# Decay and gate products in one visit, the unit's norm earlier, and matrices zeroed by GpSimd, in a two-block transformer kernel

## The reference, cut to what matters

```
r, k, v, z, wd, ad = split(token_shift(x @ w_in))
decay = exp(-exp(-softplus(-(w0 + tanh(wd) @ w_up)) - 0.5))   # decay: rank 64 up to 1024
a     = sigmoid(a0 + ad @ a_up)                               # gate: rank 64 up to 1024
kk    = normalized(k * k_k);   k = k * (1 + (a - 1) * k_a)
for t: sa = S a_t;  S = S * w_t + sa b_t + v_t k_t;  o_t = S r_t
o = (o - mean) * rsqrt(var + eps) * gn_w + gn_b               # the norm, head by head
o = (o + sum(r * k * r_k) * v) * silu(z)
```

## Time and profile before

| what | value |
|---|---|
| median of three runs | 3003.76 us (3002.83 to 3004.73) |
| the profiled execution's own time | 3004.44 us |
| its span | 3002.6 us |
| PE busy | 2942.5 us, 98% |
| DVE, ACT, POOL busy | 1686.2, 1247.3, 279.7 us |
| granted TensorE clock, mean | 0.994 |

### The profile page before, as it was taken

The page is one execution under the profiler, slowest core; times in us unless marked ns, Lnnn a source line. Parts: engine busy times, 40 slices in busy tenths (PEclk is TensorE's granted clock), DMA queues, the critical chain, the costliest instruction groups (busy, mean ns, idle before and its releaser), DMA issues.

```text
span 3002.6 us, 39945 instructions
## 1 busy us (share of the span) xinstructions
PE 2942.5 (98%) x15626; PEld 2367.6 (79%) x15626; DVE 1686.2 (56%) x3028; ACT 1247.3 (42%) x2193; POOL 279.7 (9%) x513
## 2 busy tenths in 40 slices
PE   8999999999999999999999999999999999999997
PEld 7878878787878887777778877877878787787886
DVE  6555555545453335565653346666666666666557
ACT  5444443434333325454443234343444434344322
POOL 0110100001000000000000002020120202023101
PEclk9999999999999999999999999999999999999999
DMA  4222222222233322222233323132222313126244
GB/s 171 79 85 78 85 78 84 84 79 84 80 124 134 119 97 72 77 72 71 71 109 140 128 92 93 57 95 73 83 87 71 100 57 101 62 88 204 80 153 155
DMA packets 86794, 289.16 MB, mean 96 GB/s; under 512 B 12096, under 2 KB 12864, under 8 KB 86352
## 3 DMA queue, kind: packets, MB, share of 16 engines
q1 hardware_dynamic: 71184, 246.42, 24.2%
q0 software_dynamic: 15424, 40.19, 4.4%
HBM read 261.26 MB, written 25.17 MB: 95 GB/s over the span
## 4 chain that ended last, share of the span: by engine, by line
PE 92%; DVE 4%; ACT 2%; issue 2%; DMA 0%; DVEq 0%; ACTq 0%
PE bank L283 18%; PE bank L285 17%; PE bank L284 17%; PE bank L287 7%; PE bank L289 7%; PE bank L288 7%; PE bank L1383 2%; PE bank L340 1%; PE bank L320 1%; PE bank L1292 1%; PE bank L469 1%; PE bank L482 1%; PE bank L1313 1%; PE bank L1320 1%; ACT mc_split L566 1%
## 5 line engine op out<-in xcount | busy, mean ns | idle before, releaser
L283 PE MATMUL bank<-ma_split,mc_split 128*128 128x512 f32 x2304 | 954.6, 414 | 22.9 <-DVE mb L1807 14.2
L736 DVE TENSOR_TENSOR mc_split<-mc,mc_split 128x1024 fp32r<-128x1024 f32 x434 | 534.8, 1233 | 766.4 <-ACT mc_split L566 765.6
L285 PE MATMUL bank<-ma_split,mc_split 128*128 128x512 f32 x2304 | 904.3, 392 | 0.0
L284 PE MATMUL bank<-ma_split,mc_split 128*128 128x512 f32 x2304 | 902.0, 391 | 0.0
L566 ACT ACTIVATE mc_split<-mc 128x1024 fp32r<-128x1024 f32 x434 | 457.2, 1055 | 583.7 <-PE bank L287 321.3
L283 PEld LDWEIGHTS bank<-ma_split,mc_split 128*128 128x128 f32 x2304 | 435.1, 189 | 132.9 <-issue 58.4
L285 PEld LDWEIGHTS bank<-ma_split,mc_split 128*128 128x128 f32 x2304 | 434.0, 188 | 96.1
L284 PEld LDWEIGHTS bank<-ma_split,mc_split 128*128 128x128 f32 x2304 | 436.1, 189 | 80.0 <-issue 5.5
L287 PE MATMUL bank<-mc_split,ma_split 128*128 128x512 f32 x576 | 232.0, 403 | 4.0 <-DVE mb L1807 2.4
L289 PE MATMUL bank<-mc_split,ma_split 128*128 128x512 f32 x576 | 225.5, 392 | 0.0
L288 PE MATMUL bank<-mc_split,ma_split 128*128 128x512 f32 x576 | 225.1, 391 | 0.0
(11 more groups left out here) (366 smaller groups left out, 3605.4 us busy)
## 6 DMA issues: line engine op xcount, KB each, us to landing
mc<-in_w SPq DMA_DIRECT2D x434, 512.0 KB, 3.6
x<-mc POOLq DMA_DIRECT2D x8, 1024.0 KB, 5.2
y<-mb_split SPq DMA_DIRECT2D x28, 256.0 KB, 2.6
ma_split<-y POOLq DMA_DIRECT2D x28, 256.0 KB, 4.6
mb<-in_xt SPq DMA_DIRECT2D x8, 512.0 KB, 8.9
mc<-in_x POOLq DMA_DIRECT2D x4, 1024.0 KB, 5.5
mc<-x POOLq DMA_DIRECT2D x4, 1024.0 KB, 7.7
mats<-mc POOLq DMA_DIRECT2D x32, 128.0 KB, 2.2
```

The source lines that it names most:

```text
L283: mm = pe.matmul(banks[j][:], wh[:, c], act_hi[:, kt, :], start=(kt == kts[0]), stop=False)
L284: pe.matmul(banks[j][:], wl[:, c], act_hi[:, kt, :], start=False, stop=False)
L285: last = pe.matmul(banks[j][:], wh[:, c], act_lo[:, kt, :], start=False, stop=(kt == kts[-1]))
L736: dve.tensor_tensor(w_low[:, s % NR, :, :], w_raw[:, s % NR, :, :], w_high[:, s % NH, :, :].bitcast(F32), ALU.subtract).then_inc(w_lo, 1)
```

## The change

Four edits:

1. Step k = 0 of a unit issues both products, decay into bank 7 and gate into bank 4; step k = 1 keeps only ACT's part, which reads bank 4.
2. The state's U product goes to columns 256 to 383 of bank 6 in place of bank 4, which frees bank 4 for the gate.
3. The norm's steps 36 to 41 of units 0 to 6 stand at points 164, 167, 175, 180, 183 and 186 in place of 178, 181, 184, 187, 190 and 193. For the last HGRN head, steps up to m = 8 take the other heads' spacing of 4.5 points, and the later ones stand 4 points behind where they stood.
4. `m8` is zeroed by GpSimd at the start of its second program, behind a wait for the row norms (`rb_ready`), in place of DVE in unit 0.

```diff
-                return begin + 178 + 3 * (i - CHUNK_K)
+                return begin + (164, 167, 175, 180, 183, 186)[i - CHUNK_K]
             def hg_at(h, m):
-                return 128 * h + 65 + m * (40 if h == UNITS - 1 else 45) // 10
+                if h == UNITS - 1 and m > 8:
+                    return 128 * h + 101 + 4 * (m - 8)
+                return 128 * h + 65 + 9 * m // 2
...
-            D_BANK = banks[7]
+            D_BANK, A_BANK = banks[7], banks[4]
...
-                CHUNK += [(f"R{c}", 6, "act")] * (c > 0) + [(f"U{c}", 4, "dve"), (f"O{c}", 5, "act")]
+                CHUNK += [(f"R{c}", 6, "act")] * (c > 0) + [(f"U{c}", 6, "dve"), (f"O{c}", 5, "act")]
...
-            C_BANK = {name: banks[b] for name, b, _ in CHUNK if b}
+            C_BANK = {name: banks[b][:, 2 * P:3 * P] if name[0] == "U" else banks[b] for name, b, _ in CHUNK}
...
-                if ("rw", k) in D_USES:
+                if ("rw", k) in D_USES and k != 1:
                     d_claim(pe, "rw", u, k)
-                if k in (0, 1):
+                if k == 0:
                     if u == 0:
                         pe.wait_ge(wa_ready, 2)
-                    rank = slice(k * RANK, (k + 1) * RANK)
-                    pe.matmul(D_BANK[:], up[rank, cols], wa[rank, :], start=True, stop=True).then_inc(d_done, 1)
+                    for i, bank in enumerate((D_BANK, A_BANK)):
+                        rank = slice(i * RANK, (i + 1) * RANK)
+                        pe.matmul(bank[:], up[rank, cols], wa[rank, :], start=True, stop=True).then_inc(d_done, 1)
...
-                    act.activation(asg, D_BANK[:], ACT.Sigmoid, bias=pc[A0]).then_inc(d_free, 1)
+                    act.activation(asg, A_BANK[:], ACT.Sigmoid, bias=pc[A0]).then_inc(d_free, 1)
...
-                        dve.memset(m8, 0.0).then_inc(m8_zeroed, 1)
...
             def second_pool(pool):
+                pool.wait_ge(rb_ready, 3)
+                pool.memset(m8, 0.0).then_inc(m8_zeroed, 1)
                 pool.wait_ge(m8_zeroed, 1)
```

## The result

The changed kernel takes 2962.34 us, the median of four runs (2958.5 to 2964.83), against 3004.24 us for the kernel before (3002.83 to 3006.88). The ratio is 0.9858, with a 95% interval of 0.9841 to 0.9875: 42 us faster. The forecast was 2970 us with a range from 2965.5 to 2982. The profiled execution took 2963.0 us, its span is 2961.2 us.

The account below looks back on a forecast made before the run. The prediction took TensorE, busy 98% of the span, as the bound: its instructions plus its holes. Terms of 9.1 + 17.7 + 1.0 + 4.4 + 3.1 - 1.2 = 34.1 us gave 2970 us, range 2965.5 to 2982.

Parts of the forecast that it names:

- decay and gate together: In 8 units, one visit for both products costs what one did, saving 1.14 us each: 9.1 us gained.
- holes at seven block ends: At seven hg block ends, the earlier norm closes TensorE's 2.52 us wait for emptied banks: 17.7 us gained.
- the wait of L1241 behind them: TensorE's wait for the fourth bank, four times, 2.0 us in all, mostly closes: 1.0 us gained.
- unit 0: Without DVE's 3.47 us memset, the waits of L1262 and L1241 in unit 0 go: 4.4 us gained, lower end 2.3.
- last head's product: L1383's 2.9 us wait for L1828 at the last head closes with its step 4 points later: 3.1 us gained.
- wait for the inverses: TensorE waits up to 0.5 us for GpSimd's inverses in each of units 1 to 6: 1.2 us lost.
- rival of three passes: Strict program order makes the merged visit one pass longer: 4.2 us, 2974.5 us; half or no overlap together 0.09.
- the walk: New order traced through hg block 3: emptying starts near 2234.6, bank 0 free near 2235.3, about 0.5 us to spare.
- late-split rival: At block ends the last split still waits for ACT, so 7.8 us of holes stay: 2978 us, chance 0.10.
- the slower one: The norm does not fit DVE's 4.64 us idle mid-block, delaying the first chunk matrices' copies: about 3010 us, chance 0.03.
- What is late next: The inverses GpSimd sends: 2.3 us slack in unit 6, holes removed ahead of them, so it waits 0.5 us.
- every mishap that the rivals named: GpSimd's chain late (2976 to 2979 us, 0.17), late split (2978, 0.10), half or no overlap (2974.5 or 2979.4, 0.09).

Follow-up runs that it names:

- The holes put back: Changed kernel with 5, 10, 15 or 25 small DVE memsets ahead of the emptying of the banks in blocks 1 to 7: 2970.77, 2981.24, 2992.67, 3015.49 us.
- first row: Changed kernel with five small DVE memsets ahead of the emptying of the banks in blocks 1 to 7, 0.6 us idle at each end: 2970.77 us.
- a_samehalf: Changed kernel with the gate product reading the decay's rows, so both products lie on one half of TensorE's array: 2969.19 us, ratio 0.9884.
- a_head: Changed kernel with the last HGRN head's steps back at their old points: 2961.37 us, ratio 0.9860 to the kernel before.
- b_norm: Kernel before with only the norm's new points added: 2977.36 us, ratio 0.9913, 26.4 us faster than before.
- a_memset: Changed kernel with the matrices (m8) zeroed by DVE again in place of GpSimd: 2966.78 us, ratio 0.9875.

## Why the prediction was wrong

**Where it failed: the sum.** It priced a hole of TensorE at its idle time and 0.16 us, and had no term for the clock behind it: falls of the clock were put at nothing without a reason, and those that went, less the one that came, measured 7.8 us. The mean granted clock of the kernel before, 0.994, stood in the table of times; in which stretches it fell the prediction did not ask. Counted over the same large matmuls in both traces, the terms are:

| term | forecast | measured in the two traces |
|---|---|---|
| decay and gate together | 9.1 | 10.1 |
| holes at seven block ends | 17.7 | 17.7 |
| the wait of L1241 behind them | 1.0 | 2.2 |
| unit 0 | 4.4 | 4.4 |
| last head's product | 3.1 | 3.1 |
| wait for the inverses | -1.2 (six units) | -2.9 (unit 7 alone) |
| falls of the clock, those gone less the one that came | none | 7.8 |
| sum | 34.1 | 42.4 |

The falls are 4.6 us at three block ends, 1.7 in unit 0 and 3.0 at the last head (6.8 us at half clock, of which 0.4 still lie in the hole), less 1.5 in unit 7 of the changed kernel. The traces' own difference is 41.4 us; the first part, which no edit touches, ran 1.0 us longer in the changed kernel's profile, so the terms add up. Without the clock they come to 34.6 us, close to the forecast, but in part by luck: visits and L1241 gave 2.2 us more than forecast, and the inverses took 1.7 more. The holes put back show that the clock term is a cause and not an accident of two profiles: the time grows by more than the idle, by 1.1 to 1.6 us for each 3.4 us at half clock that the traces have (6 us for 17.1, 11 for 23.9, 15 for 47.8), and in the changed kernel it grows with the idle alone where no fall follows (first row).

**Decay and gate.** The mechanism was right: L1292 was the right row, and a_samehalf shows that the two halves of the array carry the gain. The size was off by 0.10 us a visit: the second large matmul behind one starts that much later, and the earlier trace rows ended a row too early to show it. The rival of three passes was read into the Trainium skill, "TensorE: Matmul & The Clock Gate", section "The mechanism", which has matmuls start and end strictly in program order. The trace agrees with that: the four records of a visit start at 2034.28, 2034.29, 2034.81 and 2034.82 us, and none ends before one ahead of it. What failed was the prediction's own assumption that both passes of decay stand ahead of both of gate. They go in pairs, and the row of L1256 shows the time of two passes.

**The norm.** All steps of the walk came out: transposes, ACT, the split, the emptying with 0.7 us to spare (0.5 forecast), and DVE's idle time took the norm. The late-split rival and the slower one did not happen.

**Unit 0 and the last head.** The 4.4 us of unit 0 came. GpSimd's memset took 3.52 us, within the 3.5 to 5.3 forecast, and was over 15 us before the lanes start, so it cost nothing. The last head's 3.1 us came too, but a_head shows that this edit is worth nothing beside the rest.

**What is late next.** Right in kind, wrong in place. I had six units waiting up to 0.5 us, taking the chain's length as fixed. It got shorter: in unit 3 the transfer of the sub-blocks (L2037, issued at 2231.6) took 5.8 us to land before, and 4.3 now (L2040, issued at 2213.3). The view of each line in that unit, before and after:

```profile
DMA to landing us min/median/max: 5.8/5.8/5.8
```

```profile
DMA to landing us min/median/max: 4.3/4.3/4.3
```

What goes beside it has moved: before, two stores of the HGRN output and a load of weights were issued within 1 us behind it; now these three are issued 0.5 to 1.3 us ahead of it, and two further stores 1.4 us behind. That these slow it was not tried by itself. The inverses in unit 6 landed after 4.8 us instead of 5.9. Unit 7 I left out: before, its transfer was issued at 2788.6, landed 5.4 us later, and the transposes began at 2803.4, 9.4 us of slack. The prediction did not ask what filled it: a hole of 2.5 us, one of 3.1, and 6.8 us at half clock (3.0 us lost), all of which the change removed. With that, the chain also became longer: 1.4 us between the last matrix sent and the issue of the inverses, and 1.0 us in their transfer, which landed after 6.4 us. And the head's product that stood ahead of the transposes, 0.8 us of TensorE's time, stands behind them now. Together these are the 9.4 us of slack and the new wait of 2.7, 12 us in all.

**The range.** It took in every mishap that the rivals named, on the slow side, and nothing on the fast side. The lower end came from each term at its best, but a missing term has no best.

## What to carry to other kernels

When a change removes holes of TensorE, read the granted clock around each hole first. Here a hole of 1.9 us or more could be followed by a stretch at half clock, which cost 1.5 us and was not there every time, so a forecast needs a term for it and a wider range on both sides. Slack that stands behind a transfer may consist of the very holes that the change removes; take them off first, and then ask which transfers will meet. And two products with a contraction of 64 are best issued in one visit, on the two halves of the array; here they went into two banks, and one bank was not tried.

## What the runs showed of the hardware

The clock was not expected: after 0.6 us of idle no fall in seven, after 1.9 us four, after 3.2 us seven (3.4 us each), after 5.9 us seven of 6.8 us each. With 2.4 us it was three of seven in one kernel and five of seven in another. But length alone does not decide: holes of 2.8 us in b_norm (two) and a_head, and one of 3.4 us in a_memset, had no fall behind them. Matmuls of 64 rows on different halves of the array ran fully side by side, although each is made of two passes: four passes in 1.13 us, against 1.98 us on one half. Behind any visit, or a hole, the second large matmul starts late: 0.33 us after the first behind a visit with 64 rows, 0.31 behind one with 128 rows (L1383 before, 2806.09 and 2806.40 us) or a hole (2238.30 and 2238.61), in place of 0.23. A visit with 64 rows also starts late: 0.32 us after the large matmul ahead of it, where L1383 starts after 0.23.
